# A fourth accumulating transfer per group for the sums of weights

## The reference

```python
def swiglu(x, w_gate, w_up, w_down):
    return (jax.nn.silu(x @ w_gate) * (x @ w_up)) @ w_down

for i in range(DEPTH):                      # DEPTH = 2
    h = rmsnorm(x, g_ffn1_pre[i])
    x = x + 0.5 * rmsnorm(swiglu(h, w1_gate[i], w1_up[i], w1_down[i]), g_ffn1_post[i])
    ...                                     # mixing
    h = rmsnorm(x, g_ffn2_pre[i])
    x = x + 0.5 * rmsnorm(swiglu(h, w2_gate[i], w2_up[i], w2_down[i]), g_ffn2_post[i])
```

## Time and profile before

| | us |
|---|---|
| three runs | 2776.00, 2776.38, 2776.91 (median 2776.38) |
| the profiled execution | 2777.24 |
| its span, first to last instruction | 2775.3 |
| PE busy | 2766.6 |
| DVE busy | 1788.8 |
| ACT busy | 1404.6 |
| POOL busy | 99.4 |

### The profile page before, as it was taken

The page is one execution under the profiler, slowest core; times in us unless marked ns, Lnnn a source line. Parts: engine busy times, 40 slices in busy tenths (PEclk is TensorE's granted clock), DMA queues, the critical chain, the costliest instruction groups (busy, mean ns, idle before and its releaser), DMA issues.

```text
span 2775.3 us, 41339 instructions
## 1 busy us (share of the span) xinstructions
PE 2766.6 (100%) x16746; PEld 2434.9 (88%) x16746; DVE 1788.8 (64%) x2480; ACT 1404.6 (51%) x2188; POOL 99.4 (4%) x110
## 2 busy tenths in 40 slices
PE   9999999999999999999999999999999999999999
PEld 8998887699998899998976899988988889888888
DVE  7766466767773587763667586753866656666338
ACT  6554344565553575553536565544745535323235
POOL 0000000000100000000000000000002000000000
PEclk9999999999999999999999999999999999999999
DMA  7773323037753237743241257632242322332331
GB/s 216 176 184 108 114 62 93 25 101 196 185 142 98 84 104 193 183 131 112 73 97 39 84 153 191 160 106 99 77 108 86 99 91 80 113 97 91 114 114 61
DMA packets 158637, 321.94 MB, mean 116 GB/s; under 512 B 34417, under 2 KB 78833, under 8 KB 158449
## 3 DMA queue, kind: packets, MB, share of 16 engines
q1 hardware_dynamic: 147936, 281.55, 32.8%
q0 software_dynamic: 10368, 37.75, 8.1%
q10 hardware_dynamic: 144, 0.00, 0.0%
HBM read 315.07 MB, written 2.10 MB: 114 GB/s over the span
## 4 chain that ended last, share of the span: by engine, by line
PE 98%; DVE 1%; DMA 0%; ACT 0%; issue 0%; SPq 0%; DVEq 0%; ACTq 0%
PE banks L671 31%; PE banks L672 31%; PE banks L673 31%; PE banks L1175 1%; PE banks L1197 1%; PE banks L1234 1%; PE banks L1186 1%; PE banks L1238 0%; PE banks L1224 0%; PE banks L710 0%; PE banks L1328 0%; DMA first_raw<-in_w_up 0%; DVE PT L2780 0%; PE banks L1157 0%; PE banks L1121 0%
## 5 line engine op out<-in xcount | busy, mean ns | idle before, releaser
L671 PE MATMUL banks<-HH,WH 128*128 128x256 f32 (+2 forms) x2844 | 936.4, 329 | 0.8 <-DVE WL L2094 0.6
L672 PE MATMUL banks<-HH,WL 128*128 128x256 f32 (+2 forms) x2844 | 931.6, 328 | 0.0
L673 PE MATMUL banks<-HL,WH 128*128 128x256 f32 (+2 forms) x2844 | 931.4, 327 | 0.0
L546 DVE TENSOR_TENSOR WL<-raw,WH 128x1024 fp32r<-128x1024 f32 (+2 forms) x422 | 508.2, 1207 | 588.1 <-ACT WH L541 587.3
L541 ACT ACTIVATE WH<-raw 128x1024 fp32r<-128x1024 f32 (+2 forms) x422 | 437.1, 1039 | 640.3 <-PE banks L673 404.9
L671 PEld LDWEIGHTS banks<-HH,WH 128*128 128x128 f32 x2844 | 541.0, 190 | 56.0 <-issue 7.5
L672 PEld LDWEIGHTS banks<-HH,WL 128*128 128x128 f32 x2844 | 541.1, 190 | 47.1 <-issue 1.0
L673 PEld LDWEIGHTS banks<-HL,WH 128*128 128x128 f32 x2844 | 541.0, 190 | 46.7
L671 PE MATMUL banks<-SH,WH 128*128 128x256 f32 x1152 | 326.0, 283 | 0.0
L672 PE MATMUL banks<-SH,WL 128*128 128x256 f32 x1152 | 326.0, 283 | 0.0
L673 PE MATMUL banks<-SL,WH 128*128 128x256 f32 x1152 | 326.0, 283 | 0.0
(11 more groups left out here) (316 smaller groups left out, 3334.1 us busy)
## 6 DMA issues: line engine op xcount, KB each, us to landing
raw<-in_w_down SPq DMA_DIRECT2D x112, 512.0 KB, 3.3
extra_raw<-in_w_quarters SPq DMA_DIRECT2D x96, 512.0 KB, 4.3
raw<-in_w_in SPq DMA_DIRECT2D x68, 512.0 KB, 3.7
raw<-in_w_quarters SPq DMA_DIRECT2D x60, 512.0 KB, 4.4
raw<-in_w_up SPq DMA_DIRECT2D x120, 256.0 KB, 3.0
extra_raw<-in_w_quarters POOLq DMA_DIRECT2D x36, 512.0 KB, 7.2
spare_raw<-in_w_quarters SPq DMA_DIRECT2D x24, 512.0 KB, 4.8
raw<-in_w_quarters POOLq DMA_DIRECT2D x24, 512.0 KB, 6.9
```

The source lines that it names most:

```text
L546: e.tensor_tensor(WL[tile_of[u]][:, 0:n], raw[raw_of(u)][:, 0:n], WH[tile_of[u]][:, 0:n].bitcast(F32), ALU.subtract).then_inc(*low.done((u,)))
L671: e.matmul(o, wh, ah, start=start, stop=False, skip_group_check=skip)
L672: e.matmul(o, wl, ah, start=False, stop=False, skip_group_check=skip)
L673: return e.matmul(o, wh, al, start=False, stop=stop, skip_group_check=skip)
```

## The change

The addition of b21 to the buffer "sum" moves from DVE to a third accumulating transfer of the group (the fourth sum of weights). POOL issues it once the low part of product 2 has been split off, that is when nothing reads the running sum any more, and the split of product 6 waits for its landing. Since the quarter b21 is then read from HBM a second time, its buffer is free after the split of product 3, and `FREED` hands it on earlier.

```diff
-FREED = ("b11", "third", "b22", "b21", "sum")
+FREED = ("b11", "b21", "third", "b22", "sum")
@@ slot_free
             s, g, q = key
-            if q == "b21":
-                return vec.at("weight_sum", s, g, 6)
-            return low.at(W[s, "seven", g, {"b11": 0, "third": 4, "b22": 5, "sum": 6}[q]])
+            return low.at(W[s, "seven", g, {"b11": 0, "b21": 3, "third": 4, "b22": 5, "sum": 6}[q]])
@@ split_high
-                elif ph in (2, 6):
-                    e.wait_ge(*vec.at("weight_sum", s, g, ph))
+                elif ph == 2:
+                    e.wait_ge(*vec.at("weight_sum", s, g))
+                elif ph == 6:
+                    e.wait_ge(*added["sum"].at("fourth", s, g))
@@ vector_seven
                 split_low(e, W[s, "seven", g, 5])
-                vector_weight_sum(e, s, g, 6)
                 split_low(e, W[s, "seven", g, 6])
@@ gpsimd_weight_sums
                     e.wait_ge(*quarter_landed(s, g, q))
-                    if g > SEVEN_GROUPS[0]:
-                        e.wait_ge(*added[q].at(s, g - 1))
-                    elif s:
-                        e.wait_ge(*added[q].at(s - 2, SEVEN_GROUPS[-1]))
+                    before = (s, g - 1) if g > SEVEN_GROUPS[0] else (s - 2, SEVEN_GROUPS[-1])
+                    if before[0] >= 0:
+                        e.wait_ge(*(added[q].at("fourth", *before) if q == "sum" else added[q].at(*before)))
                     e.dma_start(raw_quarter(s, g, q)[:], W.quarter(s, g, other), accum_op=ALU.add).then_inc(
                         *added[q].done((s, g)))
+                e.wait_ge(*low.at(W[s, "seven", g, 2]))
+                e.wait_ge(*added["sum"].at(s, g))
+                e.dma_start(raw_quarter(s, g, "sum")[:], W.quarter(s, g, (1, 0)), accum_op=ALU.add).then_inc(
+                    *added["sum"].done(("fourth", s, g)))
```

More of the change, by code:

```diff
@@ L2279, in vector_sum_low, with vector_weight_sum @@
                 *vec.done(("input_low", s, i)))
-        def vector_weight_sum(e, s, g, ph):
+        def vector_weight_sum(e, s, g):
             if g > SEVEN_GROUPS[-1]:
                 return
-            other = {2: "b22", 6: "b21"}[ph]
-            e.wait_ge(*quarter_landed(s, g, other))
+            e.wait_ge(*quarter_landed(s, g, "b22"))
             target = raw_quarter(s, g, "sum")
-            e.tensor_tensor(target[:], target[:], raw_quarter(s, g, other)[:], ALU.add).then_inc(*vec.done(
-                ("weight_sum", s, g, ph)))
+            e.tensor_tensor(target[:], target[:], raw_quarter(s, g, "b22")[:], ALU.add).then_inc(*vec.done(
+                ("weight_sum", s, g)))
         def vector_gate_scale(e, s, g, j):
@@ L2354, in vector_seven @@
                     if i:
-                        vector_weight_sum(e, s, 2, 2)
+                        vector_weight_sum(e, s, 2)
                     vector_sum_low(e, s, 2 + i)
@@ L2378, in vector_seven @@
                     vector_hidden_low(e, s, 1)
-                vector_weight_sum(e, s, g + 1, 2)
+                vector_weight_sum(e, s, g + 1)
                 vector_c12(e, s, g)
```

## The result

| | before | changed |
|---|---|---|
| median of the runs, us | 2776.61 (2776.00 to 2776.91, 4 runs) | 2805.66 (2794.98 to 2805.96, 4 runs) |
| ratio | | 1.0095, 95% interval 1.0077 to 1.0113 |
| profiled execution: span, us | 2775.3 | 2804.1 |

The changed kernel is 29 us slower by the medians; the ratio goes by the means, in which the one run of 2794.98 counts. The forecast was 2776.4, that is no change, with a range up to 2783; the median lies 23 us above that range. A second set of runs of the same changed kernel gave 2807.34 (2803.39 to 2808.77, 4 runs; ratio 1.0107, 1.0092 to 1.0122).

What follows compares the result with a forecast made beforehand. PE was taken to bound the kernel. Removed work, fourth transfer, POOL and SP each added 0 to the profiled 2777.24 us, so the median forecast was 2776.4 us, range 2774.4 to 2783.

Steps and rivals of the forecast that it cites:

- What bounds the kernel before: PE, busy 2766.6 of 2775.3 us, sets the time; the other engines matter only if something PE needs comes late.
- What is removed: 36 additions on DVE, 43.9 us of its busy time; PE waits for none of it, so worth 0.
- The fourth transfer and its wait: Before the split of product 6: 12.3 us available, longest measured landing 9.1 us, so cost 0.
- What is moved on POOL: Sum of group 7 starts at 133.8 instead of 132.42, lands by 142.9 or 146.0, needed at 146.5; cost 0.
- What is moved on SP: Three loads per group start earlier, that of "third" by 1.2 us; even the slowest pair is 0.5 us early; cost 0.
- What it adds on the DMA engines: Share rises by 0.15 to about 0.90; landings grow by 1 to 2 us, which the available time takes.
- The rivals: Slow chain of "third" 0.07, late fourth transfer 0.06, isolated lateness at a stage's first group 0.05, faster 0.03.
- the chain of "third": Load, transfer and splits of "third" become the bound as the DMA share stretches them: 30 us slower, 2806; chance 0.07.

Runs made afterwards that it cites:

- Experiment 1: Changed kernel, but the fourth transfer counts its own semaphore, so the next sum transfer no longer waits for its landing: 2776.66 us, ratio 0.9999 to before.
- experiment 5: Changed kernel, loading only half the columns of b21 and third from group 4 of a stage on (output incomplete): 2776.97 us, ratio 1.0000.
- experiment 4: Changed kernel with the old order of handing on buffers (b11, third, b22, b21, sum): 2799.16 us, ratio 1.0081.
- experiment 2: Kernel before, no transfer added, the next group's sum transfer issued only after the low split of product 6: 2916.42 us, ratio 1.0498.
- experiment 6: Changed kernel, with POOL issuing the fourth transfer after the low split of product 3 instead of product 2: 2882.12 us, ratio 1.0378.

## Why the prediction was wrong

**What bounds the kernel before:** right. Experiments 1 and 5 have the fourth transfer on the DMA engines and lie at 2777, as long as nothing reaches PE.

**What is removed:** right, worth 0. DVE's busy time fell by 40.9 us (43.9 forecast) and PE gained nothing from it.

**The fourth transfer and its wait:** right. It lands after 5.4 us (median; 6.8 most), well inside the 12.3 us, and ACT's split of product 6 in group 5 came at 120.15 in place of 121.20.

**What is moved on POOL: this step failed.** I priced only what the order of the queue does to the sum of group 7: 133.8 us, behind the wait for the low split. I left out the second wait of the same instruction, for the landing of the fourth transfer, which the diff and the waits printed with the order both show (`s_weights_added_sum`). It was issued at 138.70, and landed 9.0 us later, at 147.7, where the latest landing that I had allowed was 146.0, for a split at 146.5. The 3.1 us that I had allowed for the transfer in front was the time that it holds the engines; the wait goes on until it has landed, 5.8 us from issue to issue (132.86 to 138.70). Experiment 1, without that wait, has it at 133.97, where I had put it. And I compared each landing with a deadline on PE's clock, one group at a time, as "so many us early". For the sum transfer that is the wrong question, since its deadline itself moves: the low split of product 2 that releases the next fourth transfer waits, through the split of product 1, for this sum. The step had to be closed to a loop: 5.4 + 0.6 + 8.6 + 1.1 + 1.1 + 0.7 + 1.1 + 0.6 + 0.8 + 1.2 + 0.4 = 21.6 against 20.16. With before's median of 6.8 for the sum it would have been 19.8: I could have seen that only 0.4 us were left. That median mixes "sum" and "third": before, the sum transfers alone had a median of 5.5 us, and with it the loop is 18.5. Closing the loop would thus have shown the danger, but not by itself the loss; it took the growth of the sum transfer as well.

**What is moved on SP:** right. The third of group 6 was issued by POOL at 125.97 (125.0 forecast, 126.15 before), and its chain made nobody late. One thing I did not ask is whether the new order of the loads lengthens the sum transfers; the first stage of experiment 4 suggests that it can, its other stages do not, and it stays open.

**What it adds on the DMA engines:** the share rose to 0.82 to 0.85 (0.90 forecast) and the medians of all loads and of line 3050 grew by 1.1 and 0.8 us (1 to 2 estimated). But the sum transfers, which the loop goes through, grew from 5.5 to 8.2 us (medians), up to 10.1: this term was too small. The growth is harmless by itself (experiment 1) and is the second condition of the loss.

**The rivals:** the chain of "third" was priced at 2806, by chance the measured time. The kind was right (a loop through a transfer that is longer than 20.16 us), the place wrong: its transfers are not those on the chain of waits.

No kernel here beats both: experiment 1 is as fast as before (0.9999), since PE is the bound in both.

## What to carry to other kernels

An added wait is priced twice: once against the deadline of its own group, and once around the loop that it closes, from the waiting instruction through all that follows back to itself one turn later; the sum is compared with the bound engine's time for a turn. Look at what an issue waits for beyond its place in the queue: transfers into different buffers that count one semaphore are in series, one more semaphore made them parallel and was worth 29 us here. The early turns of a trace do not acquit such a loop: here three of them took 20.16 us with sum transfers of 6.1 to 6.3 us, and the loop passed PE's turn only when one took 9.0; a loop that is a little too long also has slack to eat before it shows.

## What the runs showed of the hardware

An accumulating transfer of 512 KB landed after 5.4 us with no other transfer of weights in flight (kernel before, at 47.40) and after up to 11.0 us in experiment 2. Which of two successive ones is the long one differs between the kernels (changed kernel: 5.35 and 8.64; experiment 6: 7.34 and 5.39). SP's loads stand differently around them: in the changed kernel the next two were issued 2.0 and 4.2 us behind the fourth at 154.67, in experiment 6 one was issued 0.35 us ahead of the fourth at 148.92 and two more 1.9 and 3.3 us behind it. That this is the reason was not tried.

PE ran slower right behind a stall. Windows of the changed kernel in the second of the four stages, in the columns of the earlier trace rows:

```profile
725.00:730.00 5.00, 5.00 (x44) 5.00 (x43) 4.89 (x6) 1.72 (x3) 0.00 (x0) 1.00 0.22 45
730.00:735.00 5.00, 2.52 (x18) 2.34 (x17) 4.58 (x6) 4.72 (x7) 0.88 (x1) 0.91 0.53 81
735.00:740.00 5.00, 5.00 (x35) 5.00 (x34) 2.23 (x3) 1.74 (x3) 0.88 (x1) 0.75 1.03 327
```

PE stood idle for 2.5 of 5 us, and in the next 5 us its granted clock was 0.75 in the mean (0.50, the level of 1.2 GHz, from 735 to 737, and 1.00, that of 2.4 GHz, again from 738 on): 35 matmuls in place of 44 with PE busy throughout. In 160 to 200 us of the first stage, with shorter stalls, the clock stayed at 1.00. The clock over the whole run was 0.998 here, 0.988 in experiment 6 and 0.984 in experiment 2. That the slower clock lengthened a run is not shown. From 714 to 758 us the chain of waits goes round the loop and holds no matmul, so a faster PE would have waited there; and two runs of the changed kernel took 2805.84 us at a mean clock of 1.000 and 2805.96 at 0.998.
